# A two-layer decoder trunk on one core: memory keys and values in three fp32r products in place of one fp32 product

## The chip, the cores and the metric

The kernel runs on one core of a Trainium2 chip. The metric is the device time of one execution in microseconds (us), and lower is better. TensorE (PE) multiplies, VectorE (DVE) and ScalarE (ACT) do elementwise work and can read PSUM, GpSimd (Pool) does elementwise work in SBUF and issues some DMAs, SyncE (SP) issues the weight DMAs. Each engine takes its instructions strictly in program order; engines wait for each other on semaphores.

## The reference

Two layers, 256 tokens of width 1024, a memory of 256 tokens. All is fp32. The part that the change touches is the projection of the normalised memory to keys and values:

```
m = rms_norm(mem, mem_norm[l])
k, v = jnp.split(m @ wkv, 2, axis=-1)      # wkv: 1024 x 2048
k = rms_norm(k.reshape(B, MEM_LEN, XATTN_HEADS, XATTN_HEAD), k_g)
```

Around it stand, in each layer, a combined input projection, the RWKV-7 recurrence, differential attention (4 heads, two softmax maps each), an output projection, cross-attention into k and v, and a channel mixer: dense in layer 0, top-2 of 8 experts in layer 1.

## The kernel before

Weights come in blocks of 128 x 1024 fp32 (two k-tiles by 512 columns), through a ring of four SBUF slots (`ring`). SP issues the DMA of block n when slot n - 4 is free. Most blocks are multiplied in fp32r, a format of the matmul operands that keeps fewer bits than fp32. To keep precision each operand is split in a high half (`w_hi`, `h_hi`: the value rounded to fp32r, made by ACT) and a low half (`w_lo`, `h_lo`: what is left, made by DVE), and `product` (L472 to L474) issues three matmuls: high by high, low weight by high, high weight by low. There are three slots (NS = 3) of `w_hi` and `w_lo`; ACT makes the high half of block n once PE has used block n - 3.

Two kinds of block are "direct": they stay in the ring as fp32 and PE multiplies them in one fp32 matmul for each tile (L539), which the trace shows as two records. These are the blocks of the differential attention's input projection (12 a layer, lhs `xg_a` and `xg_b`) and the 16 blocks a layer of `wkv` (name `kv`, lhs `mem_T`). A direct block frees its ring slot when PE is done with it. `mem_T` is the transposed memory times its gain, written by DVE (L1632) from PSUM.

The order of work is written by hand. PE runs the recurrence in two token tiles, t = 0 and t = 1. Each tile has five levels (lv) of a triangular inverse: transposes of T (`TT`, L496), a product X (L709), another product Z (L725), each of which needs the one before it evacuated from PSUM by ACT (`TT`) or DVE (X, Z). In the gaps PE is given half a block of a projection, by the generator `project_steps`: at t = 0 blocks of the attention projection, at t = 1 blocks of kv, so kv0 and kv1 ahead of the levels, kv2 to kv6 in the five levels, two halves each. Then kv7 to kv15 lie between the steps of the differential attention, two a head. The memory is transposed at t = 0, in the state phase behind the levels (two parts, p = 0 and p = 1), and its gain applied by DVE there.

In each engine's program `ahead(name)` inserts the weight splits that may stand in front of the evacuation of `name`: as many blocks as PE has taken by that bank, plus NS. DVE also works through `side_step`, pieces of the attention's norms, inside the levels, and through group norms inside the attention.

## Time and profile before

| | |
|---|---|
| median of 3 runs | 1915.58 us (1913.62 to 1916.8) |
| profiled execution, its own time | 1913.58 us |
| its span, first to last instruction | 1911.7 us |
| mean granted TensorE clock | 0.986 |
| kv blocks of layer 0 on PE | about 154 to 249 us |
| kv blocks of layer 1 on PE | about 689 to 784 us |
| expert loop | about 900 us to the end |

Times in a row are in us from the start of the span; in a group of the page they are busy time in total and ns for one.

### The profile page before, as it was taken

The numbers are of one execution on the slowest core, as the hardware profiler recorded it, in microseconds if no ns is written. First come the engines' busy times: TensorE is split into PE (matmuls) and PEld (weight loads), VectorE is DVE, ScalarE is ACT, GpSimd is POOL, SyncE is SP. The second block draws the span as 40 slices with busy tenths as digits, with TensorE's granted clock in tenths as the row PEclk, the third lists the DMA queues.
The fourth block names the chain that finished last, engine by engine and source line by source line (L and its number), as shares of the span: only waits on it lengthen the run. The fifth ranks groups of instructions, "written<-read, shape, count | busy, mean of one in ns | idle before, by whom it ended". The sixth has DMA issues, their size and how long they took to land.

```text
span 1911.7 us, 31576 instructions
## 1 busy us (share of the span) xinstructions
PE 1825.6 (95%) x10589; PEld 1418.7 (74%) x10589; DVE 1492.5 (78%) x2051; ACT 1172.8 (61%) x1576; POOL 74.6 (4%) x110
## 2 busy tenths in 40 slices
PE   6899998999988999988999999999999999999998
PEld 5555577888865565677788888888888888888886
DVE  5854776655567556765999999989999999999997
ACT  4432454554544123453887787887787788877875
POOL 4100000000030000000200000000000000000000
PEclk9999999999999999998999999999999999999999
DMA  8431262665653322534999999999999999999993
GB/s 260 153 107 62 80 207 89 189 187 187 188 154 118 120 64 68 165 110 165 325 381 337 362 361 348 370 338 362 356 347 369 352 348 381 332 364 348 361 370 140
DMA packets 224012, 474.51 MB, mean 248 GB/s; under 512 B 16680, under 2 KB 41400, under 8 KB 223376
## 3 DMA queue, kind: packets, MB, share of 16 engines
q1 hardware_dynamic: 219456, 458.29, 68.2%
q0 software_dynamic: 3472, 13.65, 2.2%
q8 instruction: 55, 0.90, 0.2%
q10 hardware_dynamic: 960, 1.10, 0.2%
q14 instruction: 69, 0.57, 0.1%
HBM read 468.25 MB, written 1.05 MB: 245 GB/s over the span
## 4 chain that ended last, share of the span: by engine, by line
PE 54%; DVE 1%; issue 0%; ACT 0%; DVEq 0%
PE psum L472 16%; PE psum L474 16%; PE psum L473 16%; PE psum L1012 2%; PE psum L1059 1%; PE psum L1023 0%; PE psum L1024 0%; PE psum L883 0%; PE psum L871 0%; PE psum L496 0%; ACT hN L1287 0%; PE psum L581 0%; ACT SH L1479 0%; PE psum L1104 0%; DVE x L2236 0%
## 5 line engine op out<-in xcount | busy, mean ns | idle before, releaser
L472 PE MATMUL psum<-w_hi,h_hi 128*128 128x512 f32 (+1 forms) x1552 | 613.2, 395 | 33.2 <-DVE w_lo L426 26.6
L474 PE MATMUL psum<-w_hi,h_lo 128*128 128x512 f32 (+1 forms) x1552 | 605.6, 390 | 0.0
L473 PE MATMUL psum<-w_lo,h_hi 128*128 128x512 f32 (+1 forms) x1552 | 605.4, 390 | 0.0
L472 PEld LDWEIGHTS psum<-w_hi,h_hi 128*128 128x128 f32 x1552 | 293.9, 189 | 103.1 <-DVE w_lo L426 21.1
L474 PEld LDWEIGHTS psum<-w_hi,h_lo 128*128 128x128 f32 x1552 | 293.8, 189 | 62.5
L473 PEld LDWEIGHTS psum<-w_lo,h_hi 128*128 128x128 f32 x1552 | 294.4, 190 | 59.0 <-issue 0.2
L426 DVE SCALAR_TENSOR_TENSOR w_lo<-ring,col,w_hi 128x512 fp32r<-128x512 f32 (+1 forms) x184 | 130.9, 758 | 77.1 <-ACT w_hi L412 76.2
L442 DVE TENSOR_TENSOR w_lo<-ring,w_hi 128x1024 fp32r<-128x1024 f32 x144 | 172.4, 1221 | 7.6 <-ACT w_hi L438 3.2
L438 ACT ACTIVATE w_hi<-ring 128x1024 fp32r<-128x1024 f32 x144 | 151.9, 1060 | 41.0 <-PE psum L474 41.0
L412 ACT ACTIVATE w_hi<-ring,col 128x512 fp32r<-128x512 f32 (+1 forms) x184 | 118.7, 697 | 94.4 <-PE psum L474 76.5
L442 DVE TENSOR_TENSOR w_lo<-dproj,w_hi 128x1024 fp32r<-128x1024 f32 x120 | 145.9, 1222 | 17.3 <-ACT w_hi L438 14.0
L438 ACT ACTIVATE w_hi<-dproj 128x1024 fp32r<-128x1024 f32 x120 | 127.9, 1066 | 36.2 <-PE psum L474 36.2
L442 DVE TENSOR_TENSOR w_lo<-SH,w_hi 128x1024 fp32r<-128x1024 f32 x120 | 144.0, 1222 | 6.3 <-ACT w_hi L438 4.1
L438 ACT ACTIVATE w_hi<-SH 128x1024 fp32r<-128x1024 f32 x120 | 127.7, 1064 | 23.4 <-PE psum L474 23.0
L472 PE MATMUL psum<-h_hi 128*128 128x512 f32 x336 | 137.1, 408 | 0.1
L474 PE MATMUL psum<-h_hi,h_lo 128*128 128x512 f32 x336 | 131.6, 392 | 0.0
L473 PE MATMUL psum<-h_lo,h_hi 128*128 128x512 f32 x336 | 131.1, 390 | 0.0
L442 DVE TENSOR_TENSOR w_lo<-proj,w_hi 128x1024 fp32r<-128x1024 f32 x96 | 115.3, 1221 | 6.8 <-ACT w_hi L438 5.3
L539 PE MATMUL psum<-ring,mem_T 128*128 128x512 f32 x256 | 119.7, 604 | 0.0
L421 DVE TENSOR_TENSOR w_lo<-ring,w_hi 128x1024 fp32r<-128x1024 f32 x54 | 65.6, 1225 | 62.8 <-ACT w_hi L407 62.6
L438 ACT ACTIVATE w_hi<-proj 128x1024 fp32r<-128x1024 f32 x96 | 101.3, 1064 | 19.1 <-PE psum L474 19.1
L407 ACT ACTIVATE w_hi<-ring 128x1024 fp32r<-128x1024 f32 x54 | 57.2, 1059 | 87.9 <-PE psum L474 74.3
(324 smaller groups left out, 2454.7 us busy)
## 6 DMA issues: line engine op xcount, KB each, us to landing
ring<-in_expert_w_gu SPq DMA_DIRECT2D x128, 512.0 KB, 5.3
SH<-in_expert_w_gu SPq DMA_DIRECT2D x120, 512.0 KB, 5.9
proj<-in_expert_w_gu SPq DMA_DIRECT2D x104, 512.0 KB, 6.3
dproj<-in_expert_w_gu SPq DMA_DIRECT2D x72, 512.0 KB, 6.0
dproj<-in_expert_w_down SPq DMA_DIRECT2D x72, 512.0 KB, 5.1
ring<-in_expert_w_down SPq DMA_DIRECT2D x64, 512.0 KB, 5.2
ring<-in_in_proj SPq DMA_DIRECT2D x48, 512.0 KB, 4.6
ring<-in_dense_w_gu SPq DMA_DIRECT2D x88, 256.0 KB, 3.1
```

The lines of the kernel that those rows point to most:

```text
L407: ins = act.activation(w_hi[:, i % NS, :], ring[:, n % RING, :], ACT.Copy)
L412: ins = act.activation(hi[:, k, :], src[:, k, :], ACT.Copy, scale=col[:, l, a + k:a + k + 1])
L421: ins = dve.tensor_tensor(w_lo[:, i % NS, :], ring[:, n % RING, :], w_hi[:, i % NS, :].bitcast(F32), SUB)
L426: ins = dve.scalar_tensor_tensor(lo[:, k, :], src[:, k, :], col[:, l, a + k:a + k + 1], hi[:, k, :].bitcast(F32), MUL, SUB)
L438: act.activation(hi_e[j % NS_E], ring_e[j % RING_E], ACT.Copy).then_inc(hi_done, 1)
L442: dve.tensor_tensor(lo_e[j % NS_E], ring_e[j % RING_E], hi_e[j % NS_E].bitcast(F32), SUB).then_inc(lo_done, 1)
L472: pe.matmul(o, h[0], w[0], start=start, stop=False, skip_group_check=True)
L473: pe.matmul(o, h[0], w[1], start=False, stop=False, skip_group_check=True)
L474: return pe.matmul(o, h[1], w[0], start=False, stop=stop, skip_group_check=True)
L539: last = pe.matmul(banks[c][t][:, 0:cw], lhs, wd[:, k, :], start=(kb + k == 0), stop=(kb + k == 7), skip_group_check=True)
L1012: last = pe.matmul(bank[:, k * P:(k + 1) * P], hNv[:, t, (4 * g + k) * P:(4 * g + k + 1) * P], Psel[:, t, :], start=(t == 0), stop=(t == 1))
L1059: last = pe.transpose(bank[:, k * P:(k + 1) * P], act[:, c % 2, k * P:(k + 1) * P], ident)
```

## The change

The 32 kv blocks (16 a layer) are no longer direct. ACT makes their high half as for other blocks, Pool makes their low half (`pool_lo_of`, on a semaphore of its own), and PE takes them by `product`, three fp32r matmuls for each tile. SP frees a ring slot when Pool's low half is done. The memory tile is split as well: DVE writes the gained memory to `xg_a` and `xg_b` (one instruction for g = 0, two for g = 1), waits for it and signals; ACT makes `h_hi` (`mem_hi`, behind the y1 copies of each p at t = 0), Pool makes `h_lo` and then the 16 low halves of the layer in a row. The core of the diff:

```diff
-            blocks += [("direct", src, cw, None) for _, src, cw, _ in square_blocks(wkv[l], half_chunks(4))]
+            blocks += [("pool", src, cw, None) for _, src, cw, _ in square_blocks(wkv[l], half_chunks(4))]
+        def lo_at(n):
+            if by_pool[n]:
+                return pool_lo_done, pool_no[n] + 1
+            return lo_done, split_no[n] - pool_no[n] + 1
...
-                    straight = src[0] == "mT" or name[0] == "inb"
+                    straight = name[0] == "inb"
...
                         if first and c == 0 and kb % 4 == 0:
-                            B.wait_evacuated(pe, (*src, t, kb // 4))
+                            if src[0] == "mT":
+                                pe.wait_ge(mem_split, 4 * src[1] + 2 * (kb // 4) + t + 1)
+                            else:
+                                B.wait_evacuated(pe, (*src, t, kb // 4))
...
-                    sp.wait_ge(lo_done, split_no[n - RING] + 1)
+                    sp.wait_ge(*lo_at(n - RING))
...
+            def pool_lo_of(n):
+                i = split_no[n]
+                pool.wait_ge(hi_done, i + 1)
+                pool.tensor_tensor(w_lo[:, i % NS, :], ring[:, n % RING, :], w_hi[:, i % NS, :].bitcast(F32), SUB).then_inc(pool_lo_done, 1)
...
                 pool.dma_start(mem_raw, mem_in[0].rearrange("(t p) d -> p t d", p=P)).then_inc(mem_in_s, 16)
+                for g in range(2):
+                    for t in range(TT):
+                        pool.wait_ge(mem_hi_done, 4 * l + 2 * g + t + 1)
+                        for k0, kn in ((0, 4),) if g == 0 else ((4, 2), (6, 2)):
...
+                            ins = pool.tensor_tensor(part(h_lo, g, t)[:, of, :], xgs[k0 // 6][:, k0 % 6:k0 % 6 + kn, t * P:(t + 1) * P],
+                                                     part(h_hi, g, t)[:, of, :].bitcast(F32), SUB)
+                        ins.then_inc(mem_split, 1)
+                for b_ in range(first_block[l], NPRE if l else first_block[1]):
+                    if by_pool[b_]:
+                        pool_lo_of(b_)
...
+            def mem_hi(l, g):
+                for t in range(TT):
+                    act.wait_ge(mem_gained, 4 * l + 2 * g + t + 1)
+                    for k0, kn in ((0, 4),) if g == 0 else ((4, 2), (6, 2)):
+                        ins = act.activation(part(h_hi, g, t)[:, k0 - 4 * g:k0 - 4 * g + kn, :], xgs[k0 // 6][:, k0 % 6:k0 % 6 + kn, t * P:(t + 1) * P], ACT.Copy)
+                    ins.then_inc(mem_hi_done, 1)
...
+                        if t == 0:
+                            mem_hi(l, p)
...
-                B.release(dve.tensor_tensor(memT[:, 4 * g:4 * g + 4, t * P:(t + 1) * P], four(bank),
-                                            bc(gains(l, "mem")[:, 4 * g:4 * g + 4].unsqueeze(2), 4, P), MUL), ("mT", l, t, g))
+                for k0, kn in ((0, 4),) if g == 0 else ((4, 2), (6, 2)):
+                    ins = dve.tensor_tensor(xgs[k0 // 6][:, k0 % 6:k0 % 6 + kn, t * P:(t + 1) * P], four(bank)[:, k0 - 4 * g:k0 - 4 * g + kn, :],
+                                            bc(gains(l, "mem")[:, k0:k0 + kn].unsqueeze(2), kn, P), MUL)
+                B.release(ins, ("mT", l, t, g))
+                B.wait_evacuated(dve, ("mT", l, t, g))
+                dve.engine_nop().then_inc(mem_gained, 1)
```

How instructions stand on the engines. On PE, at the start of t = 1 of layer 0 (the last transpose of the recurrence's inputs, then kv0, then the first products of the tile), before:

```order
L496 MATMUL psum<-cst,NB 128x128 [waits psum_evacuated6]
L496 MATMUL psum<-cst,NB 128x128 x3
L539 MATMUL psum<-ring,mem_T 128x512 [waits block_in0,psum_evacuated2,psum_evacuated3]
L539 MATMUL psum<-ring,mem_T 128x512
L539 MATMUL psum<-ring,mem_T 128x512 [waits psum_evacuated3]
L539 MATMUL psum<-ring,mem_T 128x512
L669 MATMUL psum<-hN 64x128 [waits psum_evacuated6,psum_evacuated7,psum_evacuated5,psum_evacuated4]
```

and now, up to the wait for the second memory tile:

```order
L504 MATMUL psum<-cst,NB 128x128 [waits psum_evacuated6]
L504 MATMUL psum<-cst,NB 128x128 x3
L480 MATMUL psum<-w_hi,h_hi 128x512 [waits memory_weights_lo,mem_lo,psum_evacuated3,psum_evacuated2]
L481 MATMUL psum<-w_lo,h_hi 128x512
L482 MATMUL psum<-w_hi,h_lo 128x512
L480 MATMUL psum<-w_hi,h_hi 128x512
L481 MATMUL psum<-w_lo,h_hi 128x512
L482 MATMUL psum<-w_hi,h_lo 128x512
L480 MATMUL psum<-w_hi,h_hi 128x512 [waits mem_lo]
```

The four fp32 matmuls of kv0 have become twelve (nine of them shown as six and the start of the next three), and kv0 waits for Pool twice, for `memory_weights_lo` and `mem_lo`.

On Pool, from the DMA of the memory in layer 0 to the first DMA behind it; before, the first and the last row stood next to each other:

```order
L1269 DMA proj<-in_mem 128x2x1024 [waits keys_read]
L1275 TENSOR_TENSOR h_lo<-xg_a,h_hi 128x4x128 [waits mem_hi] x2
L1275 TENSOR_TENSOR h_lo<-xg_a,h_hi 128x2x128 [waits mem_hi]
L1275 TENSOR_TENSOR h_lo<-xg_b,h_hi 128x2x128
L1275 TENSOR_TENSOR h_lo<-xg_a,h_hi 128x2x128 [waits mem_hi]
L1275 TENSOR_TENSOR h_lo<-xg_b,h_hi 128x2x128
L1212 TENSOR_TENSOR w_lo<-ring,w_hi 128x1024 [waits weights_hi] x16
L1238 DMA vec<-in_vecs 128x2048 [waits y_cat_attention]
```

The low half of kv0 stands behind all six pieces of the memory's low half.

On ACT, from the copy of TT of level 1 to the copies of TT of levels 2 and 3, at t = 1 of layer 0 (the `NB` and `proj` rows are the squares and copies of the first key chunk, banks 2 and 3), before:

```order
L1283 ACTIVATE hT<-psum 128x512 [waits psum_ready4]
L1358 ACTIVATE NB,st<-psum,st 128x256 [waits psum_ready2,mem_scale_ready]
L1358 ACTIVATE NB,st<-psum,st 128x256
L1283 ACTIVATE proj<-psum,st 128x512 [waits psum_ready2]
L1358 ACTIVATE proj,st<-psum,st 128x256 [waits psum_ready3,mem_scale_ready]
L1358 ACTIVATE proj,st<-psum,st 128x256
L1283 ACTIVATE proj<-psum,st 128x512 [waits psum_ready3]
L1283 ACTIVATE hT<-psum 128x512 [waits psum_ready5]
L1283 ACTIVATE hT<-psum 128x512 [waits psum_ready6]
```

and now:

```order
L1310 ACTIVATE hT<-psum 128x512 [waits psum_ready4]
L415 ACTIVATE w_hi<-ring 128x1024 [waits block_used,block_in0]
L415 ACTIVATE w_hi<-ring 128x1024 [waits block_used,block_in1,mem_scale_ready]
L415 ACTIVATE w_hi<-ring 128x1024 [waits psum_ready3,block_in2]
L1393 ACTIVATE NB,st<-psum,st 128x256 [waits psum_ready2]
L1393 ACTIVATE NB,st<-psum,st 128x256
L1310 ACTIVATE proj<-psum,st 128x512 [waits psum_ready2]
L1393 ACTIVATE proj,st<-psum,st 128x256 [waits psum_ready3,mem_scale_ready]
L1393 ACTIVATE proj,st<-psum,st 128x256
L1310 ACTIVATE proj<-psum,st 128x512 [waits psum_ready3]
L1310 ACTIVATE hT<-psum 128x512 [waits psum_ready5]
L1310 ACTIVATE hT<-psum 128x512 [waits psum_ready6]
```

Three high halves (kv4, kv5, kv6) stand ahead of the evacuation of the key chunk, and the third waits for bank 3 to be filled, which is the end of kv3; behind them stands the copy of TT that PE's level 2 needs.

## Rows read from the trace of the kernel before

**Rows 1.** The page: busy time, and groups of part 5.
```profile
PE 1825.6 (95%) x10589; PEld 1418.7 (74%) x10589; DVE 1492.5 (78%) x2051; ACT 1172.8 (61%) x1576; POOL 74.6 (4%) x110
L539 PE MATMUL psum<-ring,mem_T 128*128 128x512 f32 x256 | 119.7, 604 | 0.0
L407 ACT ACTIVATE w_hi<-ring 128x1024 fp32r<-128x1024 f32 x54 | 57.2, 1059 | 87.9 <-PE psum L474 74.3
```
**Rows 2.** Windows, layer 0: busy PE, PEld, DVE, ACT, POOL; PEclk, DMA. Levels, attention.
```profile
166.90:194.33 27.43, 27.43 (x381) 14.71 (x379) 13.98 (x36) 6.08 (x15) 0.00 (x0) 1.00 0.31 97
208.70:250.20 41.50, 38.54 (x134) 19.36 (x132) 32.47 (x100) 23.96 (x79) 0.00 (x0) 1.00 0.34 102
```
**Rows 3.** Timeline of level 0, t = 1, layer 0: start, length, engine, instruction.
```profile
166.90 0.60 PE L496 MATMUL psum<-cst,hT 128*128 128x128 f32 x4
168.03 1.98 PE L539 MATMUL psum<-ring,mem_T 128*128 128x512 f32 x4
169.95 0.67 PE L725 MATMUL psum<-NB,hT 64*64 64x32 f32 x32
170.78 0.61 DVE L1924 TENSOR_TENSOR hT<-hT,psum 128x128 f32<-128x128 f32 x2 [0.93 <-PE psum L725]
172.37 0.60 PE L496 MATMUL psum<-cst,hT 128*128 128x128 f32 x4
```
**Rows 4.** Timeline: an fp32 block and what follows it; fp32r matmuls, twelve apart.
```profile
236.60 3.60 PE L539 MATMUL psum<-ring,mem_T 128*128 128x512 f32 x8
240.04 0.49 PE L826 MATMUL psum<-cst,SH 128*128 128x128 f32 x3
...
253.70 0.39 PE L474 MATMUL psum<-w_hi,h_lo 128*128 128x512 f32 x1
256.50 0.39 PE L474 MATMUL psum<-w_hi,h_lo 128*128 128x512 f32 x1
```
**Rows 5.** Timeline from the memory's gain to kv0 and what follows it.
```profile
150.08 1.29 DVE L1632 TENSOR_TENSOR mem_T<-psum,col 128x512 f32<-128x512 f32 x2
152.77 2.26 ACT L1283 ACTIVATE hN<-psum 128x512 f32<-128x512 f32 x4 [6.00 <-PE psum L496]
154.23 3.60 PE L539 MATMUL psum<-ring,mem_T 128*128 128x512 f32 x8
157.76 0.47 PE L669 MATMUL psum<-hN 64*64 64x128 f32 x8
```
**Rows 6.** Timeline of Pool in layer 1: two-input work at 512 and 256 columns.
```profile
543.50 1.25 POOL L1210 TENSOR_TENSOR xg_a<-h_hi,h_lo 128x512 f32<-128x512 f32 x1
552.88 0.74 POOL L1210 TENSOR_TENSOR xg_a<-h_hi,h_lo 128x256 f32<-128x256 f32 x1
```
**Rows 7.** Timeline of DVE beside that Pool work, and just after it.
```profile
541.88 6.57 DVE L426 SCALAR_TENSOR_TENSOR w_lo<-ring,col,w_hi 128x512 fp32r<-128x512 f32 x4
548.37 1.27 DVE L1623 TENSOR_TENSOR h_lo<-psum,h_hi 128x512 fp32r<-128x512 f32 x2
552.98 0.66 DVE L1574 TENSOR_TENSOR st<-st 128x2 f32<-128x2 f32 x1
555.75 0.16 DVE L1574 TENSOR_TENSOR st<-st 128x2 f32<-128x2 f32 x1
```
**Rows 8.** Timeline of ACT: first key chunk's evacuation and TT of level 2.
```profile
175.58 0.47 ACT L1358 ACTIVATE NB<-psum,st 128x256 f32<-128x256 f32 x1 [1.98 <-PE psum L539]
...
178.09 0.47 ACT L1358 ACTIVATE proj<-psum,st 128x256 f32<-128x256 f32 x1 [0.91 <-PE psum L539]
...
179.57 0.60 ACT L1283 ACTIVATE hT<-psum 128x512 f32<-128x512 f32 x1
```
**Rows 9.** Timeline of the attention: DVE's norm and row maxima, PE's waits.
```profile
218.39 0.58 DVE L1577 TENSOR_SCALAR st<-st 128x8 f32<-128x8 f32 x3
221.53 0.56 DVE L1603 TENSOR_TENSOR SH<-psum,cst 128x384 f32<-128x384 f32 x1
223.68 0.49 PE L814 MATMUL psum<-hT 64*128 64x128 f32 x4 [1.06 <-DVE SH L1603]
```

More of the change, by code:

```diff
@@ L353, in decoder_trunk @@
         direct = [b[0] == "direct" for b in blocks]
+        by_pool = [b[0] == "pool" for b in blocks]
+        pool_no = [sum(by_pool[:n]) for n in range(NPRE + 1)]
         split_no = [n - sum(direct[:n]) for n in range(NPRE + 1)]
@@ L356, in decoder_trunk @@
         NSPLIT = len(split_block)
+        NLO = NSPLIT - sum(by_pool)
+        def lo_at(n):
+            if by_pool[n]:
+                return pool_lo_done, pool_no[n] + 1
+            return lo_done, split_no[n] - pool_no[n] + 1
         arrived = [16 * sum(2 if b[0] == "gu" else 1 for b in blocks[n % RING:n + 1:RING]) for n in range(NPRE)]
@@ L382, in decoder_trunk, with splitter @@
         freed = []
-        def splitter(eng, one):
+        def splitter(eng, one, skip):
             n = [0]
@@ L389, in to @@
                 while n[0] < min(m, NPRE):
-                    if not direct[n[0]]:
+                    if not (direct[n[0]] or skip[n[0]]):
                         one(n[0])
@@ L534, in project_steps @@
                         if first and c == 0 and kb % 4 == 0:
[L535 removed]
+                            if src[0] == "mT":
+                                pe.wait_ge(mem_split, 4 * src[1] + 2 * (kb // 4) + t + 1)
+                            else:
+                                B.wait_evacuated(pe, (*src, t, kb // 4))
                         for k in range(2):
                             if straight:
[L538 to L539 removed]
+                                last = pe.matmul(banks[c][t][:, 0:cw], x_gained(kb + k, t), wd[:, k, :],
                                                  start=(kb + k == 0), stop=(kb + k == 7), skip_group_check=True)
@@ L1276, in _ @@
             act.dma_start(posi[:, :], pos_in).then_inc(small_in, 16)
-            split_to, ahead = splitter(act, lambda n: hi_of(act, n))
+            split_to, ahead = splitter(act, lambda n: hi_of(act, n), [False] * NPRE)
             def copy(dst, name, src=None, scale=1.0, func=ACT.Copy, more=0):
@@ L1595, in rsqrt @@
                 return y if to is None else to
-            split_to, ahead = splitter(dve, lambda n: lo_of(dve, n))
+            split_to, ahead = splitter(dve, lambda n: lo_of(dve, n), by_pool)
             def evac(dst, name, src, other, op, more=0):
```

14 lines of the change are left out of this document (6 added, 8 removed).

## The prediction

> **What bounds the kernel now.** I read the page first [rows 1]: PE is busy for 1825.6 us of 1911.7, DVE for 1492.5, ACT for 1172.8, Pool for 74.6. The kv matmuls are 256 records, 119.7 us of PE. Averages don't say what kv is worth, so I took the windows around it [rows 2]. In the five levels of t = 1 PE is busy all the time (27.43 of 27.43 us) and DVE half of it (13.98). In the attention PE has 38.54 of 41.50 us, DVE 32.47 (78%), ACT 23.96. The timeline of a level shows who waits [rows 3]: from one transpose of T to the next it takes 172.37 - 166.90 = 5.47 us, the kv halves lie in it back to back with the products, and DVE idles 0.93 us for PE. So the levels are bound by PE, kv included. In the attention it is mixed: PE waits 1.06 us for DVE's row maximum [rows 9], and between 218.39 and 221.53 DVE is in a chain of tiny norm operations that the next row maximum stands behind.
>
> **Step 1, the products.** An fp32 block runs from 236.60 to the next instruction at 240.04: 3.44 us. Twelve fp32r matmuls take 256.50 - 253.70 = 2.80 us [rows 4]. So a block saves 0.64 us, 16 blocks 10.2 us a layer, 20.5 us in all, if PE is the bound everywhere and nothing is late. That is the whole prize.
>
> **Step 2, the start of kv.** Today DVE ends the last gain at 150.08 + 1.29 = 151.37, and PE takes kv0 at 154.23, as cover for ACT's four copies (152.77 to 155.03) [rows 5]. Now the chain is: gain in two pieces with a wait and a signal, which I put at 0.9 us a tile, so the last tile is ready at about 152.5; ACT's high half of it to 153.4; Pool's low halves; and only then Pool's low half of kv0, because it stands behind all six pieces. Pool takes 1.25 us for 512 columns of two inputs and 0.74 for 256 [rows 6]: 0.51 us for 256 columns more, so 1024 columns cost 1.25 + 2 x 0.51 = 2.27 us. The trace has no Pool instruction of that size; the lower bound is the 1.25 of the 512, the upper one three times 1.25, 3.75. Pool runs the third tile from 152.5 to 154.0, the fourth to 155.5, kv0 to 157.8. PE starts 3.6 us late, and the first products of the tile at 157.8 + 2.80 = 160.6 where they were at 157.76. At the bounds the wait is 2.6 or 5.1. It is paid twice: +7.2 us.
>
> **Step 3, ACT's queue.** ACT gets 16 high halves a layer of 1.06 us [rows 1]. Most fall in its idle time (6.08 of 27.43 us busy in the levels [rows 2]). One does not. Ahead of the evacuation of the first key chunk stand kv4, kv5 and kv6, and kv6 waits for the end of kv3. Today ACT takes that chunk in two parts from 175.58, the first while PE still multiplies the second, and copies TT of level 2 from 179.57 [rows 8], hidden by PE's half block. Now nothing starts until kv3 is done: 1.06 for the high half, then the two parts, which take 179.57 - 175.58 - 0.91 = 3.1 us without the wait between them, 0.6 for TT, with hand-overs 5.0 us. PE meanwhile has 168.03 - 166.90 = 1.13 us of transposes and products [rows 3] and a half block of 1.40, 2.5 us. It waits about 2.4 us: +4.8 in two layers.
>
> **Step 4, where the saving meets another engine.** In level 4 PE already waits for DVE copies, so one half saves nothing (0.3). In the attention two high halves (kv10, kv11) come ahead of an exponential and an attention output; each sets ACT back by 1 us, and DVE, which has no slack there, with it. Of the 9 x 0.64 = 5.8 us that nine blocks could save in the attention I expect 2. High halves in the state phase add 0.5. Together +4.6 a layer, +9.2.
>
> Steps 1 to 4 give -20.5 + 7.2 + 4.8 + 9.2 = +0.7 us: the change has about paid for itself.
>
> **Step 5, Pool against DVE.** In layer 1 Pool works from 543.50 to 555.7. Beside it DVE's split of 128x512 takes 6.57 / 4 = 1.64 us, where the memory's gain of the same shape, with one input in PSUM, takes 1.29 / 2 = 0.65 [rows 5]. A 128x2 operation takes 0.66 us beside Pool and 0.16 just after it [rows 7]. A tiny operation has no data to be slow on: it waits for the running Pool instruction to end, and 0.5 us is what is left of one of 0.74. Operations with one input in PSUM (L1623, 1.27 for two) are not slower. So each Pool instruction of 2.27 us can hold a DVE instruction with two SBUF inputs for up to 2.27 us, on average half of it. The Trainium skill has this too: "GPSIMD Engine Reference", section 1, says that Pool's SBUF interfaces are shared with VectorE, with contention for DVE instructions that have two SBUF inputs or run in a two-port mode. By that rule the low halves would slow what DVE does beside them; the trace agrees, 0.66 against 0.16 us. Whoever drops the page loses nothing of the sum.
>
> Which ones meet? In the levels DVE evacuates from PSUM and has 13 us free, so kv3 to kv6 cost little; kv7 can meet the SBUF copies of level 4 (up to 2.3). In the state phase kv8 and kv9 meet the scaling of the state and the side steps that stand ahead of the next evacuation (1 to 2). In the attention kv10 to kv13 meet the row maxima and the norm chain from 218.39 to 221.53 [rows 9], some eleven tiny instructions: the first waits for what is left of a Pool instruction, and a second may catch the rest. Six blocks of up to 2.27 are 13.6 us at most; half is 6.8, and PE's own work covers a part. I take 3.5 for the attention, 1 for level 4 and 1.5 for the state: 6 us a layer, +12. The bounds are 0 (they all miss each other) and 11 a layer: 7 for the attention, 2.3 for level 4, 2 for the state.
>
> **Sum.** +0.7 + 12 = +12.7 us on the profiled execution's 1913.58, 1926.3. The profiled execution is 2.0 below the median of 1915.58, so against the runs 1928.3; I say 1928.
>
> Hidden and not priced: DMA. SP now frees a slot when the low half is done, which is earlier than when PE is done, except for kv4, so the ring is no later. If that cover failed a landing of some 4 us would show as ACT's wait at a high half. The 3.6 us without a product at kv0 may also let the granted clock fall: PEclk is 1.00 in both windows [rows 2], and I add nothing.
>
> **Rivals.**
>
> *A, the other side: the saving comes through.* PE is the bound and DVE's slack swallows Pool's holds. What speaks for it: the levels at 100% PE; DVE idle half of the time. Against it: DVE's 78% in the attention and steps 2 and 3, which come from program order alone. Then steps 1 to 3 with 1 us a layer of step 4: -20.5 + 7.2 + 4.8 + 2 = -6.5, 1909. It decides once holds and queues of steps 4 and 5 stay under 4.2 us a layer; with Pool at its lower bound of 1.25 us it would be 1907.
>
> *B, waits and gain cancel.* Step 5 is near nothing, since the norm chain and the Pool instructions miss each other, and step 4 is as I have it: +0.7, 1916.
>
> *C, full contention.* Each low half meets a DVE chain, 11 us a layer, and the holds set PE idle long enough to lower the clock; 22 + 0.7 and some 3: 1941.
>
> *D, Pool becomes the bound.* Pool would then be near 100% busy in the attention. At 2.27 us a block against at least 2.80 of PE it doesn't; it would from about 3.5 us on, which is within the upper bound of step 2. Part of C.
>
> **How the numbers follow.** Forecast 0.52 (1919 to 1937 by itself, the bounds of step 5 halved), A 0.20, B 0.15, C with D 0.13. What a measurement of this kernel can tell from no change is 0.2%, 3.8 us. The forecast is slower but for its lowest edge (0.03 same), B is same (0.11) with a tail each side (0.02 each), A is faster but for 0.02, C is slower: faster 0.20, same 0.16, slower 0.64. The range takes A's centre and C's: 1908 to 1942.
>
> **What would show it.** In the changed kernel's trace: kv blocks of 2.80 us pitch (step 1); PE idle 3 to 4 us ahead of the first kv product at t = 1, released by Pool (step 2); PE's Z product of level 2 waiting for ACT's copy of TT (step 3); Pool at about 2.3 us a low half and some 42 us more a layer (36 for the weights, 5.5 for the memory); DVE's tiny norm operations in the attention with one of 1 to 2 us among them, and the row maximum of head 2 some us late (step 5). Wrong would be: Pool's 1024 columns much under 2 us, DVE operations of their old length beside Pool, or a level that gets shorter by the full 0.64 us with the attention shorter too. Then A holds.

## The result, and the profile after

| | before | after |
|---|---|---|
| median (lowest to highest), 4 runs each | 1915.42 us (1913.62 to 1916.8) | 1954.67 us (1950.81 to 1957.38) |
| ratio | | 1.0202, 95% interval 1.0188 to 1.0216 |
| profiled execution: span | 1911.7 us | 1955.5 us |
| mean granted clock | 0.986 | 0.968 |

The change costs 39 us. The forecast was +12.7 us, with a range up to 1942: the direction was right, the size was three times too small, and the time lies outside the range.

The page of the changed kernel, busy time and the groups that answer to [rows 1]:

```profile
PE 1833.5 (94%) x10717; PEld 1466.2 (75%) x10717; DVE 1533.3 (78%) x2055; ACT 1208.8 (62%) x1620; POOL 165.2 (8%) x154
L1212 POOL TENSOR_TENSOR w_lo<-ring,w_hi 128x1024 fp32r<-128x1024 f32 x32 | 79.9, 2508 | 131.2 <-ACT w_hi L415 131.1
```

DVE has 1533.3 us busy where it had 1492.5, although it was given almost nothing to do (the memory's gain in six pieces in place of four). PE has 8 us more, although its products became shorter. PE's idle time, span less busy, went from 1911.7 - 1825.6 = 86.1 us to 122.0.

The windows of layer 0, columns as in [rows 2]. The first line is the state phase of the kernel before, which lies between the two windows of [rows 2]; the other three are the levels, the state phase and the attention of the changed kernel, cut at the same products of PE as in the kernel before:

```profile
194.33:206.22 11.89, 9.97 (x274) 9.27 (x273) 5.98 (x12) 6.49 (x13) 0.00 (x0) 1.00 0.14 48
166.84:198.49 31.65, 25.89 (x401) 19.38 (x400) 20.29 (x36) 10.70 (x20) 12.85 (x5) 0.95 0.26 81
198.49:216.43 17.94, 13.12 (x272) 12.38 (x272) 9.17 (x12) 8.35 (x15) 4.87 (x2) 0.71 0.21 67
218.92:270.46 51.54, 36.97 (x171) 29.00 (x169) 43.24 (x100) 29.25 (x85) 14.43 (x6) 0.87 0.27 82
```

The levels take 31.7 us in place of 27.4, the state phase 17.9 in place of 11.9, the attention 51.5 in place of 41.5. PE was never idle in the levels, and now is for 5.8 us; in the attention it is idle for 14.6 us instead of 3. The granted clock, 1.00 in all three before, is 0.95, 0.71 and 0.87. The timeline of the levels shows how the idle time arises (start, length, engine, instruction, then the idle time before it):

```profile
166.84 0.60 PE L504 MATMUL psum<-cst,hT 128*128 128x128 f32 x4
171.64 0.60 PE L504 MATMUL psum<-cst,hT 128*128 128x128 f32 x4
173.77 2.96 DVE L1611 TENSOR_TENSOR qs<-dproj,rope 128x256 f32<-128x256 f32 x2
173.90 7.53 POOL L1212 TENSOR_TENSOR w_lo<-ring,w_hi 128x1024 fp32r<-128x1024 f32 x3 [1.87 <-ACT w_hi L415]
176.76 2.46 DVE L1611 TENSOR_TENSOR dproj<-dproj,rope 128x256 f32<-128x256 f32 x1
179.25 0.61 DVE L1965 TENSOR_TENSOR hT<-hT,psum 128x128 f32<-128x128 f32 x2
179.96 0.63 PE L504 MATMUL psum<-cst,hT 128*128 128x128 f32 x4 [3.35 <-DVE hT L1965]
```

Level 0 is what was hoped for: 171.64 - 166.84 = 4.80 us from one transpose of T to the next, where it was 5.47 [rows 3]. In level 1 DVE has three 128x256 multiplications of its side step to do, 0.42 us each when alone. Beside three Pool low halves in a row one of them takes 2.5 us and one 2.46. Pool's three take 2.51 us each, so they end at 176.41, 178.92 and 181.43, and the two held instructions end at 176.73 and 179.22, 0.3 us behind the first and the second of them. The evacuation of Z, one input in PSUM and not slower at all (0.61 for two), stands behind them, and PE waits 3.35 us for it.

The attention, with the place that [rows 9] show of the kernel before:

```profile
229.40 2.54 POOL L1212 TENSOR_TENSOR w_lo<-ring,w_hi 128x1024 fp32r<-128x1024 f32 x1 [3.81 <-ACT w_hi L415]
229.61 2.77 DVE L1614 TENSOR_SCALAR st<-st 128x8 f32<-128x8 f32 x3
232.41 2.37 POOL L1212 TENSOR_TENSOR w_lo<-ring,w_hi 128x1024 fp32r<-128x1024 f32 x1 [0.47 <-ACT w_hi L415]
232.61 2.40 DVE L1617 SCALAR_TENSOR_TENSOR st<-st 128x8 f32<-128x8 f32 x2
236.97 0.56 DVE L1640 TENSOR_TENSOR SH<-psum,cst 128x384 f32<-128x384 f32 x1
239.12 0.80 PE L824 MATMUL psum<-hT 64*128 64x128 f32 x4 [7.61 <-DVE SH L1640]
241.72 0.63 PE L482 MATMUL psum<-w_hi,h_lo 128*128 128x512 f32 x1
244.01 0.39 PE L480 MATMUL psum<-w_hi,h_hi 128*128 128x512 f32 x1
```

The chain of tiny norm operations meets two Pool instructions and is held by both: three that took 0.58 us take 2.77, two of 0.37 take 2.40. PE waits 7.61 us for the row maximum behind them, where it waited 1.06. When it gets going it is at 1.2 GHz: fp32r products begin every 0.43 us (241.29, 241.72, 242.14), and from 243.31 on every 0.23. So here an idle stretch is paid a second time.

### The profile page after: what moved, and what is told of

The parts are those of the page before. It is cut to its first block, busy times and chain, and to the rows that moved or that the text cites. A ratio compares the mean times of both kernels' runs of the same rounds, so it can differ in the third digit from the quotient of the medians.

```text
span 1955.5 us, 31958 instructions
## 1 busy us (share of the span) xinstructions
PE 1833.5 (94%) x10717; PEld 1466.2 (75%) x10717; DVE 1533.3 (78%) x2055; ACT 1208.8 (62%) x1620; POOL 165.2 (8%) x154
## 4 chain that ended last, share of the span: by engine, by line
PE 53%; DVE 0%; issue 0%; ACT 0%; DVEq 0%
PE psum L480 16%; PE psum L482 16%; PE psum L481 16%; PE psum L1022 2%; PE psum L1069 1%; PE psum L1033 0%; PE psum L1034 0%; PE psum L504 0%; PE psum L893 0%; PE psum L591 0%; PE psum L881 0%; ACT SH L1516 0%; PE psum L1114 0%; DVE x L2277 0%; DVE y_lo L2217 0%
## 5 line engine op out<-in xcount | busy, mean ns | idle before, releaser
L480 PE MATMUL psum<-w_hi,h_hi 128*128 128x512 f32 (+1 forms) x1680 | 672.8, 400 | 35.6 <-DVE w_lo L434 26.8
L481 PE MATMUL psum<-w_lo,h_hi 128*128 128x512 f32 (+1 forms) x1680 | 660.8, 393 | 0.0
L482 PE MATMUL psum<-w_hi,h_lo 128*128 128x512 f32 (+1 forms) x1680 | 660.6, 393 | 0.0
L480 PEld LDWEIGHTS psum<-w_hi,h_hi 128*128 128x128 f32 x1680 | 321.4, 191 | 113.5 <-DVE w_lo L434 23.2
L482 PEld LDWEIGHTS psum<-w_hi,h_lo 128*128 128x128 f32 x1680 | 320.8, 191 | 68.4
L481 PEld LDWEIGHTS psum<-w_lo,h_hi 128*128 128x128 f32 x1680 | 321.8, 192 | 63.3 <-issue 0.2
L446 ACT ACTIVATE w_hi<-ring 128x1024 fp32r<-128x1024 f32 x144 | 151.9, 1060 | 41.0 <-PE psum L482 41.0
L415 ACT ACTIVATE w_hi<-ring 128x1024 fp32r<-128x1024 f32 x86 | 90.6, 1058 | 105.7 <-PE psum L482 103.8
L1212 POOL TENSOR_TENSOR w_lo<-ring,w_hi 128x1024 fp32r<-128x1024 f32 x32 | 79.9, 2508 | 131.2 <-ACT w_hi L415 131.1
```

The source lines that it names most:

```text
L415: ins = act.activation(w_hi[:, i % NS, :], ring[:, n % RING, :], ACT.Copy)
L446: act.activation(hi_e[j % NS_E], ring_e[j % RING_E], ACT.Copy).then_inc(hi_done, 1)
L480: pe.matmul(o, h[0], w[0], start=start, stop=False, skip_group_check=True)
L481: pe.matmul(o, h[0], w[1], start=False, stop=False, skip_group_check=True)
L482: return pe.matmul(o, h[1], w[0], start=False, stop=stop, skip_group_check=True)
L1212: pool.tensor_tensor(w_lo[:, i % NS, :], ring[:, n % RING, :], w_hi[:, i % NS, :].bitcast(F32), SUB).then_inc(pool_lo_done, 1)
```

## The experiments

All times are medians; each ratio is to runs of the kernel before on the same chip. The runs come from several chips, so small differences are better read from the ratios. Two numbers of each kernel's profile carry most of what follows: how long DVE is busy, since a held instruction counts as busy, and how long PE is busy, since more time for the same products is time at the lower clock. Both are of one execution. In two long stretches where every kernel has the same work (from the end of layer 0's attention to the levels of layer 1's first tile, and from the end of layer 1's attention to the end) PE is busy for 372.2 to 377.5 and for 1104.7 to 1109.0 us in the profiles of eleven of these kernels; e8, which is faster than the kernel before, has 375.2 and 1108.7 where that has 372.3 and 1105.3. So up to some 9 us between two numbers of PE busy can be scatter.

| kernel | median us | ratio (95%) | DVE busy | PE busy | PE idle |
|---|---|---|---|---|---|
| before | 1912.80 to 1915.42 | 1 | 1492.5 | 1825.6 | 86.1 |
| the change | 1954.67 | 1.0202 (1.0188 to 1.0216) | 1533.3 | 1833.5 | 122.0 |
| e1 low halves by DVE | 1951.09 | 1.0190 (1.0172 to 1.0209) | 1531.0 | 1827.5 | 123.4 |
| e2 low halves left out | 1909.47 | 0.9983 (0.9968 to 0.9998) | 1494.9 | 1810.0 | 94.0 |
| e3 low halves in four | 1937.87 | 1.0132 (1.0107 to 1.0156) | 1517.2 | 1824.4 | 111.3 |
| e4 before, Pool work added | 1934.30 | 1.0101 (1.0081 to 1.0121) | 1531.4 | 1837.8 | 97.2 |
| e5 seven blocks only | 1925.13 | 1.0076 (1.0059 to 1.0093) | 1506.8 | 1825.7 | 94.7 |
| e5b seven, in four | 1922.11 | 1.0036 (1.0020 to 1.0052) | 1498.4 | 1826.6 | 93.7 |
| e6 low halves of nine | 1942.78 | 1.0154 (1.0137 to 1.0171) | 1523.9 | 1828.2 | 114.0 |
| e7 one-input Pool work | 1930.39 | 1.0099 (1.0082 to 1.0116) | 1514.2 | 1832.3 | 95.4 |
| e8 seven, by DVE, ordered | 1907.11 | 0.9969 (0.9955 to 0.9983) | 1510.9 | 1823.6 | 83.7 |
| e9 all, by DVE, ordered | 1924.57 | 1.0067 (1.0044 to 1.0090) | 1533.4 | 1814.2 | 108.1 |
| e10 e2 with ACT reordered | 1904.29 | 0.9950 (0.9934 to 0.9965) | 1494.5 | 1809.6 | 92.7 |
| e11 the change, ACT reordered | 1958.96 | 1.0240 (1.0217 to 1.0263) | 1532.8 | 1817.4 | 121.5 |

### e2 and e4: the Pool work taken away, and the Pool work alone

e2 cuts each weight low half on Pool to eight columns:

```diff
-                pool.tensor_tensor(w_lo[:, i % NS, :], ring[:, n % RING, :], w_hi[:, i % NS, :].bitcast(F32), SUB).then_inc(pool_lo_done, 1)
+                pool.tensor_tensor(w_lo[:, i % NS, 0:8], ring[:, n % RING, 0:8], w_hi[:, i % NS, 0:8].bitcast(F32), SUB).then_inc(pool_lo_done, 1)
```

> The changed kernel with Pool's kv low halves cut to 8 of their 1024 columns: the rest of w_lo keeps old data, so keys and values are not computed fully. All waits, ACT's high halves, the twelve products and the order of work stay. This is steps 1 to 4 of the prediction without step 5. Theory (Pool holds DVE): steps 1 to 4 gave +0.7 us with 3.6 us of late start a layer, of which the profile of the changed kernel shows 1.3; without the low half of kv0 on the way it is less still. Expected 1907 us, between 1900 and 1917. Rival (program order, ACT's high halves, the products' clock): 1945 or above. Rival in between (the hold is half of it): about 1930.

e4 is the kernel before with as many Pool instructions, for which nothing waits:

```diff
+                for b_ in range(first_block[l] + 28, first_block[l] + 44):
+                    pool.wait_ge(*freed[max(b_ - 2, first_block[l] + 28)][0:2])
+                    step(pool.tensor_tensor(xg_a[:, 0:1024], xg_a[:, 0:1024], vec[:, 0:1024], ADD))
```

> The kernel before, with 16 Pool instructions a layer added that do nothing useful: 128x1024, two SBUF inputs, each once PE has used the kv block two before it (three of them at kv0). Everything else is the kernel before: fp32 products, no high halves, nothing waits for Pool. Theory (the running Pool instruction holds DVE): +30 us, since the saving of the products isn't there but the start and ACT's part aren't either: 1945, between 1930 and 1960, with the granted clock down as in the changed kernel. Rival (the loss is in the program order and the products): 1915 to 1919.

Measured: 1909.5 and 1934.3. Both lie in the ranges of the theory of the hold; e4 is 11 us under its centre, and its mean granted clock is 0.980, not down to the 0.968 of the changed kernel. Program order, high halves and products are cleared of the loss, since e2 has them all and is a little faster than before. That also answers the rival named with e1, that fp32r products by themselves lower the clock: e2 has the same products at 0.985. e4 shows in undisturbed surroundings which instructions are held. Its timeline in layer 0:

```profile
157.77 7.20 POOL L1256 TENSOR_TENSOR xg_a<-xg_a,vec 128x1024 f32<-128x1024 f32 x3 [66.27 <-PE psum L539]
158.95 2.87 DVE L1606 TENSOR_TENSOR SH<-psum,masks 128x512 f32<-128x512 f32 x4 [5.42 <-PE psum L669]
162.77 2.76 DVE L1900 TENSOR_TENSOR hT<-hT,masks 128x512 f32<-128x512 f32 x1
...
212.85 2.64 POOL L1256 TENSOR_TENSOR xg_a<-xg_a,vec 128x1024 f32<-128x1024 f32 x1 [15.80 <-PE psum L539]
214.11 0.42 DVE L1967 TENSOR_REDUCE st<-SH 128x1 f32<-128x256 f32 x1
214.56 0.97 DVE L1968 TENSOR_SCALAR st<-st 128x2 f32<-128x2 f32 x1
```

Four evacuations from PSUM beside Pool keep their 2.87 us. The multiplication of hT by the masks, both in SBUF, takes 2.76 in place of 0.69: it starts at 162.77 and ends 0.56 after Pool's at 164.97. A reduction of SBUF data keeps its 0.42. A TENSOR_SCALAR on two columns, 0.17 alone, takes 0.97 and ends at 215.53, with Pool's at 215.49. The Trainium skill has this rule on the page "SBUF — State Buffer", section "Who interferes with whom": a DVE instruction with two SBUF inputs and a GpSimd instruction that reads SBUF contend, so do a tensor_scalar or copy in a two-port mode and GpSimd; whichever is first keeps the shared ports for its whole length; and on this chip a reduction never contends. The traces of this Pool instruction agree, 0.97 against 0.17 us and 0.42 against 0.42. A copy of 64x256 in SBUF, 0.30 us in e2, takes 2.49 in level 4 of the change, beside a low half of 2.39.

The sum over the program: DVE is busy for 1531.4 - 1492.5 = 38.9 us more in e4, and for 1533.3 - 1494.9 = 38.4 more in the change than in e2. That is 1.2 us for each of 32 Pool instructions of about 2.4, half of one, in both. What differs is what becomes of it: +20 us of time in the kernel before, 1954.67 - 1909.47 = +45 in the changed one. In e4 the row maximum of head 2 alone makes PE wait 5.89 us, where it waited 1.06:

```profile
222.70 2.34 POOL L1256 TENSOR_TENSOR xg_a<-xg_a,vec 128x1024 f32<-128x1024 f32 x1 [1.74 <-PE psum L539]
222.84 2.43 DVE L1583 SCALAR_TENSOR_TENSOR st<-st 128x8 f32<-128x8 f32 x2
228.78 0.80 PE L814 MATMUL psum<-hT 64*128 64x128 f32 x4 [5.89 <-DVE SH L1606]
```

### e3, e7: how long one hold is

e3 makes each low half in four instructions of 256 columns:

```diff
-                pool.tensor_tensor(w_lo[:, i % NS, :], ring[:, n % RING, :], w_hi[:, i % NS, :].bitcast(F32), SUB).then_inc(pool_lo_done, 1)
+                for q in range(4):
+                    s = slice(256 * q, 256 * q + 256)
+                    ins = pool.tensor_tensor(w_lo[:, i % NS, s], ring[:, n % RING, s], w_hi[:, i % NS, s].bitcast(F32), SUB)
+                ins.then_inc(pool_lo_done, 1)
```

> The changed kernel with each kv low half on Pool in four instructions of 256 columns in place of one of 1024. By the 0.72 us of a 256-column piece of the memory's low half, a block takes some 2.9 us of Pool in place of 2.5. Theory as the prediction had it (a DVE instruction waits for the end of the Pool instruction that runs, then goes on): the hold falls from up to 2.5 us to up to 0.75 us for each, but there are four times as many to meet; a chain of tiny instructions loses 0.7 us at most for each. Expected 1940 us, between 1928 and 1950. Rival (the two engines share the port at a given rate, or Pool keeps it over a row of instructions): 1955 or more, since Pool is at work for longer. Rival (Pool's lateness counts, not the hold): Pool is later by 0.4 us a block, 1960.

Measured 1937.9. The group on the page:

```profile
L1214 POOL TENSOR_TENSOR w_lo<-ring,w_hi 128x256 fp32r<-128x256 f32 x128 | 100.1, 818 | 97.2 <-ACT w_hi L415 97.2
```

and the timeline of level 1, the same place as above:

```profile
178.53 1.30 DVE L1614 TENSOR_TENSOR qs<-dproj,rope 128x256 f32<-128x256 f32 x2
178.66 4.03 POOL L1214 TENSOR_TENSOR w_lo<-ring,w_hi 128x256 fp32r<-128x256 f32 x5 [1.46 <-ACT w_hi L415]
```

Pool works 20 us longer in all, and still the kernel is faster, by 17 us in the medians and 0.7% (13 us) in the ratios: what counts here is how long a Pool instruction is, not how long Pool works. DVE's pair takes 1.30 us, not 2.96, and DVE is busy for 16 us less over the program.

e7 is e4 with two Pool instructions of one SBUF input each in place of every added one:

```diff
-                    step(pool.tensor_tensor(xg_a[:, 0:1024], xg_a[:, 0:1024], vec[:, 0:1024], ADD))
+                    step(pool.tensor_scalar(xg_a[:, 0:1024], vec[:, 0:1024], 1.0, None, MUL))
+                    step(pool.tensor_scalar(xg_a[:, 0:1024], vec[:, 0:1024], 1.0, None, MUL))
```

> The kernel before with two Pool instructions in place of each of the 16 added ones a layer, that read one SBUF operand and not two (a multiplication of 128x1024 by a constant), so about the same time of Pool at work or less. With one two-input instruction each the kernel took 1934. Theory A (any Pool instruction holds DVE's until it ends): 1920 to 1935, by the length of one, and the held forms of DVE are the same as with two inputs. Theory B (only a Pool instruction with two SBUF inputs does): 1913 to 1918, and no DVE instruction of two SBUF inputs is longer than in the kernel before.

Measured 1930.4: theory B falls. But A falls in its second half too, since most of the held instructions do not wait for the end:

```profile
176.76 2.77 POOL L1257 TENSOR_SCALAR xg_a<-vec 128x1024 f32<-128x1024 f32 x1
177.76 0.42 DVE L1578 TENSOR_TENSOR dproj<-dproj,rope 128x256 f32<-128x256 f32 x1
...
215.71 2.77 POOL L1257 TENSOR_SCALAR xg_a<-vec 128x1024 f32<-128x1024 f32 x1
215.73 1.04 DVE L1969 TENSOR_SCALAR st<-st 128x2 f32<-128x2 f32 x1
...
218.56 2.77 POOL L1256 TENSOR_SCALAR xg_a<-vec 128x1024 f32<-128x1024 f32 x1
220.07 1.29 DVE L1581 TENSOR_SCALAR st<-st 128x8 f32<-128x8 f32 x3
```

A two-input DVE instruction one us into a one-input Pool instruction keeps its 0.42 us. A TENSOR_SCALAR that comes 0.02 us after its start is held for 0.87 us of its 2.77. The last two rows show a second stretch, at the end: three TENSOR_SCALARs that take 0.58 us alone take 1.29, up to 221.36, where Pool's instruction ends at 221.33. Over the whole trace, beside a Pool instruction of the ordinary 2.77 us, two-input DVE instructions are held only when they begin in its first 0.9 us, and the middle of it holds nobody; some TENSOR_SCALARs and copies that begin 1.8 us or more into it are held to its end. No instruction is held for more than 0.9 us. DVE is busy for 21.7 us more, over 64 Pool instructions 0.34 each, against 1.2 for the two-input ones. The page "SBUF — State Buffer" of the Trainium skill, same section, has the engine that is first keep the shared ports for the whole instruction. This form of Pool instruction doesn't: a two-input instruction that comes in the middle, at 177.76, isn't held at all.

### e1: the low halves by DVE

```diff
-            blocks += [("pool", src, cw, None) for _, src, cw, _ in square_blocks(wkv[l], half_chunks(4))]
+            blocks += square_blocks(wkv[l], half_chunks(4))
```

> The changed kernel with the 16 kv low halves a layer made by DVE, as for the other blocks, and none of them by Pool; the memory's split stays as it is. Theory (the running Pool low half holds DVE's instructions whose operands are all in SBUF): the holds are gone, DVE has 16 instructions of about 1.22 us more a layer. In the levels it has room for them, in the attention it goes from 32.5 of 41.5 us to some 43. Expected 1912 us, between 1905 and 1925, far below the 1955 of the change. Rival (the loss comes from the program order on PE and ACT, the start of kv, and the products themselves): nothing of that moves, and the time stays at 1945 or above. Rival (the granted clock falls because fp32r products draw more): it stays about 0.968 in the mean and the attention still has stretches at half clock.

A miss: 1951.1 us, where the theory said 1912. The holds are gone, as expected (0.42 and 0.17 us for the instructions shown above), but DVE now has the low halves in its queue. They stand ahead of the memory's gain and between the evacuations of X and Z, and PE waits for them in the attention:

```profile
161.06 0.48 PE L480 MATMUL psum<-w_hi,h_hi 128*128 128x512 f32 x1
...
243.27 0.80 PE L480 MATMUL psum<-w_hi,h_hi 128*128 128x512 f32 x1 [3.03 <-DVE w_lo L429]
256.13 0.50 PE L480 MATMUL psum<-w_hi,h_hi 128*128 128x512 f32 x1 [4.52 <-DVE w_lo L429]
```

kv0 begins at 161.06, 6.8 us later than before [rows 5]. The rival named program order, and in this kernel it has a part; e2 shows that in the change itself it costs no more than the products give back. One number is worth keeping: DVE is busy for 1531.0 us here and for 1533.3 in the change. Low halves on Pool cost DVE as much, 38 us of holds, as making them itself, 32 x 1.22 = 39.

### e5, e5b, e6: where in the layer it is lost

e5 keeps kv0 to kv6 split and makes kv7 to kv15 direct again, e5b is e5 with the four pieces of e3, and e6 is the change with the edit of e2 for kv0 to kv6 alone:

```diff
+            blocks += [("pool" if q < 7 else "direct", src, cw, None) for q, (_, src, cw, _) in enumerate(square_blocks(wkv[l], half_chunks(4)))]
...
+                    straight = direct[at[0]]
...
+                m = 8 if pool_no[n] % 16 < 7 else 1024
```

> The changed kernel with only the first seven kv blocks of a layer (kv0 to kv6, those ahead of and in the levels) in fp32r, their low halves by Pool as there; kv7 to kv15 are one fp32 product again, with the gained memory in xg_a and xg_b as their left operand. In the changed kernel's trace the first scores of layer 0 stand 10.2 us later than before, and the attention adds about as much again. Theory (holds of DVE by Pool, wherever the two meet): the attention is as before and about half of the loss stays, 8 to 10 us a layer: 1930 us, between 1922 and 1938. Rival (DVE has room in the levels, so Pool costs little there, as the prediction had it): seven blocks save 0.64 us each and the start costs 1 to 2, 1910 to 1916. Rival (the attention's loss comes from the late levels alone): 1945 or above.

> The same with each of the seven low halves in four Pool instructions of 256 columns. The four pieces took 17 us off the whole change, when 16 blocks a layer were made so. Theory (a DVE instruction waits for no more than the Pool instruction in progress, and a short one is soon over): about 7 us less than with whole low halves, 1922 us, between 1912 and 1930. Rival (kv0's low half in four is later, 158.79 in place of 155.46, and that weighs more in the levels): not faster than with whole ones.

> The changed kernel with Pool's low halves of kv0 to kv6 of each layer cut to 8 of 1024 columns (the rest of w_lo is old data, keys and values are not computed fully), those of kv7 to kv15 made whole. So Pool meets DVE in level 4, the state phase and the attention only. Theory: the loss is the sum of meetings; against 1909 with none and 1955 with all, nine of 16 low halves a layer give 20 to 28 us: 1932 us, between 1925 and 1942. Rival (the attention only suffers because the levels are late): 1909 to 1918. Rival (the levels cost nothing, all is lost in the attention): 1950.

Measured 1925.1, 1922.1 and 1942.8; e6 is a little above its range. Level blocks alone cost 12 us against before in the medians, 14.5 by the ratio (1.0076), so the levels are not the free place that the prediction took them for. In e5's profile the levels are 2.0 us longer than before in layer 0 and 4.3 in layer 1, and the attention is as long as before (44.1 and 43.8 us, before 44.0 and 44.2). In e6 nine low halves a layer cost 33 us over e2, three quarters of the 45: the larger part is lost in level 4, the state phase and the attention. Four pieces gain less with seven blocks than with 16: the ratios differ by 0.4%, 1.0036 against 1.0076, which is about the 7 us expected, the medians by 3.

### e10, e11: the wait for ACT

Both move ACT's high halves from ahead of the key chunks' evacuation to behind the copy of TT; e10 in e2, e11 in the change.

```diff
-                            ahead(name)
+                            ahead(name, -NS)
...
-                        copy((kn if c < 2 else vx)[:, t, cs], name, scale=mem_r[:, t:t + 1])
+                        copy((kn if c < 2 else vx)[:, t, cs], name, scale=mem_r[:, t:t + 1], more=-NS if c < 2 else 0)
```

> The kernel whose Pool low halves are cut to 8 columns (1909 us; keys and values are not computed fully), with ACT's high halves no longer ahead of the two key chunks' evacuation but behind the copy of TT. In the trace of the kernel without this edit PE waits 2.2 and 2.0 us for ACT's copy of TT in level 2 of the two layers, and has a stretch at half clock behind it. Theory (step 3 is real and costs what the prediction gave it, 4.8 us, plus the half clock): 1903 us, between 1898 and 1906. Rival (the wait only moves to the next place): 1907 to 1911.

> The changed kernel, with Pool's low halves whole, and only ACT's high halves moved from ahead of the two key chunks to behind the copy of TT. Without Pool's low halves the same edit took 5 us off (1909.5 to 1904.3). In the changed kernel's trace PE waits 3.4 us for DVE's evacuation of Z at just that place, and the wait for ACT doesn't show. Theory (step 3's wait lies under the hold of DVE and costs nothing more): the time stays within 3 us of the change, 1952 to 1957. Rival (waits add up): 1950 or below.

The timeline of e2 in level 2 shows what step 3 described:

```profile
182.31 0.67 PE L735 MATMUL psum<-NB,hT 64*64 64x32 f32 x32 [2.21 <-ACT hT L1310]
```

e10 takes that wait away and is at 1904.3, 5 us below e2. In the change the same edit gains nothing: the median is 1959.0, 2 us above the range of the theory, and the ratio is above that of the change. Why it lies above was not looked into. Its executions lie far apart, 1940.7 and then 1956.6 to 1963.5, and the profile is of the one at 1940.7, which stands alone. Level 1 of that execution reads:

```profile
173.34 2.96 DVE L1611 TENSOR_TENSOR qs<-dproj,rope 128x256 f32<-128x256 f32 x2
173.46 2.55 POOL L1212 TENSOR_TENSOR w_lo<-ring,w_hi 128x1024 fp32r<-128x1024 f32 x1 [1.87 <-ACT w_hi L415]
176.32 0.43 DVE L1611 TENSOR_TENSOR dproj<-dproj,rope 128x256 f32<-128x256 f32 x1
177.49 0.63 PE L504 MATMUL psum<-cst,hT 128*128 128x128 f32 x4 [1.32 <-DVE hT L1965]
```

One Pool instruction stands here in place of three in a row, the third DVE instruction goes free, and PE waits 1.32 us, not 3.35. DVE is held as long over the whole program as in the change (1532.8 and 1533.3 us busy) and PE is idle as long (121.5 and 122.0); the 16.6 us between the two spans, 1938.9 and 1955.5, are 16.1 us of PE's busy time, 1817.4 and 1833.5. That is the granted clock, 0.978 and 0.968. Of the 16.1 us, 7.2 lie in the two long stretches that have the same work in every kernel, so at most 9 have to do with kv.

### e8, e9: a version that gains

e8 splits kv0 to kv6 only, makes their low halves on DVE and puts them where DVE waits for PE:

```diff
+            blocks += [("w" if q < 7 else "direct", src, cw, None) for q, (_, src, cw, _) in enumerate(square_blocks(wkv[l], half_chunks(4)))]
...
+                    if t:
+                        ahead(("m12", l, t, 0), -1)
...
-                        ahead(("X", l, t, lv, 1), -1)
                         side_step(t)
                         for par in range(2):
...
+                        ahead(("X", l, t, lv, 1), -1)
...
-                ahead(("mT", l, t, g))
+                ahead(("mT", l, t, g), -NS)
```

with ACT's order of e10. e9 does the same for all 16 blocks.

> kv0 to kv6 in fp32r, their low halves on DVE and placed where DVE waits for PE: kv0 in level 4 of t = 0, kv1 and kv2 ahead of the first products of t = 1, kv3 to kv6 behind the evacuation of Z of a level; the key chunks' evacuation on ACT no longer has high halves ahead of it; kv7 to kv15 as one fp32 product. No weight half is made by Pool, only the six pieces of the memory. Theory: a level saves its 0.64 us and DVE's 1.22 us fit in the 1.5 to 1.9 us in which it waits for the next X product; the start costs 1 to 2 us a layer. 7 x 0.64 = 4.5, less 1.5 and 0.5: 2.5 us a layer, 1909 us, between 1904 and 1916. Rival (in the levels DVE's work of two splits is on the chain wherever it stands, as in the kernel with all low halves on DVE): 1922 or above.

> The same order with all 16 kv blocks of a layer in fp32r and all low halves on DVE. With the order of the changed kernel's splitter it took 1951. The levels are as in the kernel with seven; the attention has nine low halves of 1.22 us on DVE, 11 us more on an engine with 9 us free in 41.5. Theory (the attention is then bound by DVE): 1935 us, between 1920 and 1948. Rival (most of the 1951 was lost at the start and in the levels, by order): 1915 or below.

e8 takes 1907.1 us, 0.9969 of before (0.9955 to 0.9983, 9 runs against 18): it gains some 6 us. Its levels:

```profile
165.46 0.60 PE L504 MATMUL psum<-cst,hT 128*128 128x128 f32 x4
169.01 0.61 DVE L1966 TENSOR_TENSOR hT<-hT,psum 128x128 f32<-128x128 f32 x2 [0.61 <-PE psum L735]
169.65 1.22 DVE L429 TENSOR_TENSOR w_lo<-ring,w_hi 128x1024 fp32r<-128x1024 f32 x1
170.27 0.60 PE L504 MATMUL psum<-cst,hT 128*128 128x128 f32 x4
171.51 0.49 DVE L1951 TENSOR_TENSOR NB<-psum,lower 128x128 f32<-128x128 f32 x2 [0.64 <-PE psum L719]
...
201.93 0.49 PE L824 MATMUL psum<-hT 64*128 64x128 f32 x4
```

The level takes 4.81 us; the low half fills 1.22 of the 1.86 us in which DVE would have waited; the first scores of the attention stand at 201.93, before at 206.22 and in the change at 216.43 (the line of L824 is the first product of the scores). e9 is at 1924.6, 26 us under e1 by the order of DVE's and ACT's work alone: most of e1's loss was where the low halves stood. The rest fits an attention bound by DVE (in layer 0 PE waits 4.32 us for a row maximum there, and 6.0 for low halves), but was not tried apart.

## Why the prediction went wrong, step by step

**Reading of the bounds.** Right: PE bound the levels, and a level fell from 5.47 to 4.80 us wherever DVE was left alone.

**Step 1, -20.5 us.** Right. PE's busy time in e2 is 15.6 us under that of before, with some of its products at half clock, and the level saved 0.67 us against 0.64.

**Step 2, +7.2 us.** Mechanism right, size too large. kv0 is released by Pool, but PE waited 1.31 us in layer 0 and 2.85 in layer 1, not 3.6:

```profile
149.60 0.41 DVE L1670 TENSOR_TENSOR xg_b<-psum,col 128x256 f32<-128x256 f32 x1
152.16 0.72 POOL L1275 TENSOR_TENSOR h_lo<-xg_b,h_hi 128x256 fp32r<-128x256 f32 x1
152.85 2.36 POOL L1212 TENSOR_TENSOR w_lo<-ring,w_hi 128x1024 fp32r<-128x1024 f32 x1
155.46 0.47 PE L480 MATMUL psum<-w_hi,h_hi 128*128 128x512 f32 x1 [1.31 <-POOL w_lo L1212]
158.37 2.13 PE L679 MATMUL psum<-hN 64*64 64x128 f32 x64
```

Pool's 1024 columns take 2.36 us alone, the estimate was 2.27. DVE was done with the gain at 150.0 and not at 152.5: the state phase lay 1.8 us earlier in this execution, and two pieces need 0.8 us a tile. The first products of the tile begin 0.6 us late (157.76 before), not 2.8.

**Step 3, +4.8 us.** Right where it can be seen: 2.21 and 2.0 us of waiting in e2, predicted 2.4, and 5 us in e10. In the change it lies under the longer wait for DVE and costs nothing of its own (e11).

**Step 4, +9.2 us.** Consistent as a sum; its parts were not measured. With steps 1 to 3 the prediction had +0.7 us. e2, which has no low half to wait for, measures -4.9 by the medians, and step 2 had been 3 to 5 us too large. In e10, without the wait of step 3, it is -9.3.

**Step 5, +12 us, is the step that failed.** The mechanism was right, and so was the length of the hold. "Up to 2.27 us, on average half of it" is 32 x 1.14 = 36 us over the program, measured 38.4 and 38.9. What failed is the next sentence: that the holds cost little in the levels, and that PE's own work covers part of the others, so that 12 of 36 us reach PE. Against e2 it was 45, more than all of them. The parts:

- PE's idle time is 122.0 - 94.0 = 28 us larger than in e2, not 12. The levels were expected to cost nothing, since DVE has 13 us free there. Free time on the average is no cover: what is held is the side step, and the evacuation of Z that PE waits for is next in the queue. e5 has 12 us of holds in DVE's busy time and loses 12 to 14.5 against before.
- The rest, 1833.5 - 1810.0 = 23.5 us, is PE being busy longer with the same products. This is what "I add nothing" for the granted clock left out. The windows of before had 1.00 with waits of about 1 us in them; they said nothing of waits of 3 us and more, one of which (3.6) stood in my own sum, and that unknown needed a bound and got none. The 51.5 us between the two profiled spans are those 28 and 23.5.

The two profiles are not alike in luck: e2's is its fastest execution and the change's is its slowest, and the medians are 45 us apart. So the stages around kv are worth reading apart from the rest. Lengths in us, layer 0 and layer 1, cut at the same products of PE everywhere, the attention here from its first scores on; the last column is what step 5 gave the holds, for one layer:

| stage | before | e4 | e2 | the change | step 5 |
|---|---|---|---|---|---|
| levels | 27.4, 28.7 | 27.9, 31.6 | 28.2, 28.4 | 31.7, 36.4 | 1 |
| state phase | 11.9, 10.9 | 11.9, 14.3 | 11.9, 11.0 | 17.9, 15.2 | 1.5 |
| attention | 44.0, 44.2 | 52.0, 52.1 | 41.7, 42.2 | 54.0, 48.0 | 3.5 |
| all the rest | 1744.7 | 1745.3 | 1740.7 | 1752.4 | 0 |

Over e2 the change loses 5.7 us a layer in the levels, 5.1 in the state phase and 9.1 in the attention. That is 39.8 us in two layers where step 5 had 12 and at most 22. Of them 23.0 are idle time of PE, 11.5 a layer and so already at the upper bound of 11, and 16.8 are more busy time. Another 4.2 us are the waits of kv0 for Pool, which are step 2's. The last 7.5 lie in the rest of the program, most of them in the two stretches where every kernel has the same work; by the scatter above nothing says that the change caused them.

**Why the same holds cost +20 us in the kernel before.** There PE's idle time rose by 11 us and its busy time by 12. By the table the attention loses about as much in both, 15.9 us in e4 and 18.1 in the change. The difference lies in the levels, 3.4 against 11.5, and in the state phase, 3.4 against 10.2. In the levels the added Pool instructions of e4 stood one to a level (167.06, 172.52, 177.99, 183.45), where in the change three stand in a row behind three high halves. A half block of fp32 also covers 0.3 us more of each hold than a half block of three fp32r products. Which of the two has the larger share was not separated. Nor was the full Pool work tried in e2 with nothing waiting for it: no idle buffer was found for its output. PE's waits for Pool are 1.31 and 2.85 us, so it can't be much.

**The rivals.** A, the saving comes through, is what e2, e10 and e8 do once Pool's work is gone: 1904 to 1909. B, waits and gain cancel, fell with the holds: they are not near nothing. C, full contention, came nearest: 11 us a layer and a lower clock, 1941. It was given 0.13, and it too put the clock at 3 us, where PE's busy time grew by 17 in the stages around kv. D, Pool as the bound, never came: Pool is busy for 14 of 51.5 us in the attention.

## What to carry to other kernels

Before work is moved from DVE to Pool, list the DVE instructions beside it that have two SBUF inputs, or are tensor_scalar or copy in SBUF. Here the holds came to half the length of the two-input Pool instructions, and so to as much DVE time as the moved work itself. Price the hold at what stands behind the held instruction in DVE's queue, not at DVE's average load; then price PE's idle time twice, once as waiting and once as products at 1.2 GHz behind it. Small Pool instructions (256 columns) took longer in sum and hurt less; better was to leave the work on DVE and place it where DVE waits for PE, and only in stages where it does.

## What was unexpected in the hardware

- A Pool TENSOR_SCALAR with one SBUF input, 2.77 us for 128x1024, held DVE for at most 0.9 us, at its start and for some instructions again at its end; a TENSOR_TENSOR with two, 2.36 us, from any point to its end. For the same number of elements the one-input form was the slower one.
- Two instructions that exclude each other alternated: in level 1 three Pool instructions in a row let exactly one DVE instruction of this kind pass between each two.
- With equal idle time on PE (121.5 and 122.0 us) two executions of nearly the same kernel differed by 16 us in the time of the products alone, at a mean granted clock of 0.978 and 0.968; 7 of the 16 lay in stretches of the program that have no kv work.
